# Sums of squares of eleven norms: two fp32r parts in place of one fp32 operand, in a two-block transformer kernel

## The reference

```python
def rms_norm(x, w):
    x32 = x.astype(f32)
    y = x32 * lax.rsqrt(jnp.mean(x32 * x32, axis=-1, keepdims=True) + EPS)
    return (y * w.astype(f32)).astype(x.dtype)
...
def head_rmsnorm(o, w):
    B, S, H, dv = o.shape
    of = o.astype(jnp.float32)
    y = of * lax.rsqrt(jnp.mean(of * of, axis=-1, keepdims=True) + NORM_EPS)
    return y.reshape(B, S, H * dv) * w.astype(jnp.float32)
```

## Time and profile before

| | us |
|---|---|
| median of three runs | 1858.04 |
| lowest and highest | 1856.46 and 1858.89 |
| the profiled execution | 1859.46 |
| its span | 1857.7 |
| PE busy in it | 1821.0 |

### The profile page before, as it was taken

One profiled execution on the slowest core, in us unless ns is written; L12 is line 12 of the kernel. 1 busy time (PEld: TensorE's weight loads), 2 busy tenths in 40 slices (PEclk: granted clock), 3 DMA queues, 4 the chain that ended last, 5 costly groups with the idle time before them and its releaser, 6 DMA issues.

```text
span 1857.7 us, 22226 instructions
## 1 busy us (share of the span) xinstructions
PE 1821.0 (98%) x8534; PEld 1434.4 (77%) x8534; DVE 826.2 (44%) x1381; ACT 521.2 (28%) x1038; POOL 947.5 (51%) x510
## 2 busy tenths in 40 slices
PE   7999989999999999999999999999999999999998
PEld 5885556888888887777887888677788878888886
DVE  6328754522023335435004473666645476305533
ACT  3125654221012112212104232555510132222222
POOL 5443132766666666455665555443466635444442
PEclk9999999999999999999999999999999999999999
DMA  5620101222222233121322222211122213222221
GB/s 183 212 70 26 48 23 46 102 99 94 102 91 102 91 102 113 67 81 69 110 96 75 76 73 80 68 60 69 58 102 91 102 63 107 91 102 92 101 94 65
DMA packets 46729, 162.55 MB, mean 88 GB/s; under 512 B 5392, under 2 KB 6736, under 8 KB 46241
## 3 DMA queue, kind: packets, MB, share of 16 engines
q1 hardware_dynamic: 43088, 154.52, 23.8%
q10 hardware_dynamic: 3537, 6.61, 1.2%
HBM read 158.13 MB, written 2.12 MB: 86 GB/s over the span
## 4 chain that ended last, share of the span: by engine, by line
PE 91%; DVE 4%; ACT 2%; issue 1%; DMA 0%; POOL 0%; SPq 0%; DVEq 0%; ACTq 0%; POOLq 0%
PE bank L728 90%; PE bank L1063 1%; DVE att_l_t L2048 0%; DVE att_l_t L2028 0%; DMA x_sb<-in_x 0%; DVE h_lo L1746 0%; ACT att_l_t L1561 0%; POOL w_lo_t L2295 0%; ACT sb_e L1600 0%; ACT sq L1283 0%; DVE att_l_t L2050 0%; DVE sq_sum L1692 0%; ACT sb_e L1599 0%; ACT h_hi L1392 0%; ACT att_pt L1573 0%
## 5 line engine op out<-in xcount | busy, mean ns | idle before, releaser
L2295 POOL TENSOR_TENSOR w_lo_t<-w_raw,w_hi_t 128x1024 fp32r<-128x1024 f32 x275 | 691.6, 2515 | 187.6 <-ACT w_hi_t L1359 169.7
L2293 POOL TENSOR_SCALAR w_hi_t<-w_raw 128x1024 fp32r<-128x1024 f32 x215 | 235.3, 1094 | 662.7 <-PE bank L728 633.7
L728 PE MATMUL bank<-h_hi,w_hi_t 128*128 128x512 f32 (+1 forms) x1060 | 433.4, 409 | 10.5 <-ACT h_hi L1392 9.1
L728 PE MATMUL bank<-h_hi,w_lo_t 128*128 128x512 f32 (+1 forms) x1060 | 415.2, 392 | 0.0
L728 PE MATMUL bank<-h_lo,w_hi_t 128*128 128x512 f32 (+1 forms) x1060 | 409.2, 391 | 0.4 <-DVE h_lo L1746 0.3
L728 PEld LDWEIGHTS bank<-h_hi,w_hi_t 128*128 128x128 f32 x1060 | 201.0, 190 | 70.4 <-issue 26.3
L728 PEld LDWEIGHTS bank<-h_lo,w_hi_t 128*128 128x128 f32 x1060 | 199.8, 189 | 46.2 <-issue 3.2
L728 PEld LDWEIGHTS bank<-h_hi,w_lo_t 128*128 128x128 f32 x1060 | 201.1, 190 | 40.7 <-issue 1.2
L728 PE MATMUL bank<-hid_hi,w_hi_t 128*128 128x512 f32 x432 | 168.0, 389 | 0.0
L728 PE MATMUL bank<-hid_lo,w_hi_t 128*128 128x512 f32 x432 | 168.0, 389 | 0.0
L728 PE MATMUL bank<-hid_hi,w_lo_t 128*128 128x512 f32 x432 | 168.0, 389 | 0.0
(11 more groups left out here) (308 smaller groups left out, 2676.9 us busy)
## 6 DMA issues: line engine op xcount, KB each, us to landing
w_raw<-in_w SPq DMA_DIRECT2D x276, 512.0 KB, 3.2
y<-in_w SPq DMA_DIRECT2D x6, 512.0 KB, 5.9
x_sb<-in_x SPq DMA_DIRECT2D x4, 512.0 KB, 7.7
x_sb<-in_x ACTq DMA_DIRECT2D x2, 1024.0 KB, 5.4
out_y<-x_sb SPq DMA_DIRECT2D x8, 256.0 KB, 2.1
u_raw<-in_w SPq DMA_DIRECT2D x2, 512.0 KB, 6.1
toep<-table ACTq DMA_DIRECT2D x4, 256.0 KB
decay<-in_decay SPq DMA_DIRECT2D x1, 1024.0 KB, 4.8
```

The lines of the kernel that those rows point to most:

```text
L728: return pe.matmul(out, lhs, rhs, start=start, stop=stop, **kw)
L2293: pool.tensor_scalar(hi, raw, 1.0, 0.0, ALU.mult, ALU.add).then_inc(*did("w_hi", i))
L2295: pool.tensor_tensor(lo, raw, hi.bitcast(F32), ALU.subtract).then_inc(*did("w_lo", i))
```

## The change

`IN_PARTS` names the eleven norms. For these

- DVE also adds the last square (it matters for n2 and fpre, which have eight), so that `sq_sum` is complete;
- at the step "norm" ACT copies `sq_sum` into an fp32r buffer (the high part; it uses one of the two places of `sq`), and DVE subtracts it from `sq_sum` in place (the low part);
- PE waits for the low part (`sq_lo`) and multiplies both parts by ones in fp32r into the same bank, two matmuls.

`sq_parts` is a view of the memory of `sq` and `sq_sum` with the type fp32r. ACT's next squares wait for the bank of sums where they would overwrite a high part.

```diff
--- before.py
+++ after.py
@@ -320,6 +320,7 @@
 HI_AT = {}
 for i in ACT_HI:
     HI_AT.setdefault(LAST_USE[BEHIND[i]], []).append(i)
+IN_PARTS = ("cq", "n2", "fpre") + tuple((name, h) for name in ("ret", "gla") for h in range(4))
 UNNORMED = ("n1", "n2", "pre_u", "fpre")
 FROM_U = (("rq", 0), ("rk", 0), ("rq", 1))
 FIRST_LOADS = 2
@@ -327,7 +328,7 @@
 
 SEMAPHORES = """x_in0 x_in1 x_in2 x_in3 x_back ones_set r_cols mask_in mixer_in kv_in ksw_in kr_in zeros table_out sq_pe const_in wqb_in misc_in late_in alibi_in alibi_s bias_in y_out
 w_hi wa_hi w_lo slot_used v_chain s_chain sq_s sq_v rstd rstd_used ms_lo
-h_t h_hi hy_hi u_hi h_ready x_pool p_chain bias_v bcast_v gate_v nsa_v cmpx cmp_s cmp_v att_l att_n att_exp att_p att_tr att_done
+h_t h_hi hy_hi u_hi h_ready x_pool p_chain bias_v bcast_v gate_v nsa_v sq_hi sq_lo cmpx cmp_s cmp_v att_l att_n att_exp att_p att_tr att_done
 lora mla_k mla_q mla_rot sb_sp sb_exp sb_a sb_pe conv_y y_ready p_conv hid_s hid x_ready ret_s ret_a ret_d ret_done sil
 o_ready o_hi m_ready gla_v gla_s gla_kd gla_st gla_a gla_done gla_t prod gate_s merged merged_hl q_s swa_s ft lo_t table last_t last_x""".split()
 
@@ -388,8 +389,11 @@
     par = sb("par", [P, -(-NPCOL // 32) * 32])
     small = sb("small", [P, 4, 8])
     r_col = small[:, :, 7]
-    ones = sb("ones", [P, P])
+    ones_r = sb("ones", [P, P], F32R)
+    ones = ones_r[:].bitcast(F32)
     ident = sb("ident", [P, P])
+    with nc.sbuf_tensor("sq_parts", [P, 3, T], F32R) as sq_r:
+        pass
     sq = sb("sq", [P, 2, T])
     sq_sum = sb("sq_sum", [P, T])
     rstd_t = sb("rstd_t", [P, 3, T])
@@ -620,6 +624,9 @@
         if step[0] == "sq":
             sq_use[step[1:]] = len(sq_use)
     sq_uses = list(sq_use)
+
+    def sum_high(key):
+        return sq_r[:, sq_use[(key, len(norms[key][0]) - 2)] % 2]
 
     def rstd(key):
         _, parts, cols, *_ = norms[key]
@@ -757,6 +764,11 @@
                                              False, True))
                 return
             out = take(("ms", key))
+            if key in IN_PARTS:
+                pe.wait_ge(*after("sq_lo", key))
+                mm(out[:], ones_r[:], sum_high(key), True, False)
+                fill(("ms", key), mm(out[:], ones_r[:], sq_r[:, 2], False, True))
+                return
             if n_src == 1:
                 pe.wait_ge(*after("sq_s", key, 0))
                 rhs = sq[0:parts, sq_use[(key, 0)] % 2, 0:cols]
@@ -1255,7 +1267,7 @@
             u = sq_use[(key, c)]
             if u >= 2:
                 k2, c2 = sq_uses[u - 2]
-                if len(norms[k2][0]) == 1 or c2 == KD - 1:
+                if len(norms[k2][0]) == 1 or c2 == KD - 1 or (k2 in IN_PARTS and k2 != key):
                     act.wait_ge(*ms_full(k2))
                 else:
                     act.wait_ge(*after("sq_v", k2, max(c2, 1)))
@@ -1323,6 +1335,9 @@
                     act.wait_ge(*evacuated(("ms", key, hf)))
                     act.activation(r_half, r_half, ACT.Exp, scale=-0.5).then_inc(*did("rstd", key, hf))
                 return
+            if key in IN_PARTS:
+                act.wait_ge(*after("sq_v", key, len(srcs) - 1))
+                act.activation(sum_high(key), sq_sum[:], ACT.Copy).then_inc(*did("sq_hi", key))
             act.wait_ge(*full(("ms", key)))
             r = ring_at.get(key, 0)
             if r >= 3:
@@ -1679,7 +1694,7 @@
         def squares(key, c):
 
             srcs, parts, cols, *_ = norms[key]
-            if 0 < c < KD - 1:
+            if 0 < c < KD - (key not in IN_PARTS):
                 own("sq_s", key, c)
                 b = [sq[0:parts, sq_use[(key, x)] % 2, 0:cols] for x in (c - 1, c)]
                 if c == 1:
@@ -1715,7 +1730,12 @@
         last_h = None
         for step in ORDER:
             stage = step[0]
-            if stage == "bias_tables":
+            if stage == "norm" and step[1] in IN_PARTS:
+                key = step[1]
+                own("sq_hi", key)
+                dve.tensor_tensor(sq_r[:, 2], sq_sum[:], sum_high(key).bitcast(F32), ALU.subtract)\
+                   .then_inc(*did("sq_lo", key))
+            elif stage == "bias_tables":
                 dve.memset(y[:, 5:8], 0.0).then_inc(*did("zeros"))
                 for n, (c0, w) in enumerate(TAB):
                     dve.wait_ge(*full(("tab", n)))
```

## The result

| | before | changed |
|---|---|---|
| median, us | 1857.25 | 1898.9 |
| lowest and highest | 1856.38 and 1858.89 | 1897.28 and 1901.24 |
| span of the profiled execution | 1857.7 | 1899.4 |

The changed kernel is slower by 2.25%: the ratio is 1.0225, with a 95% interval of 1.0212 to 1.0238, or 41.7 us between the medians. The forecast was 1904, in a range of 1886 to 1918.

What follows compares the result with a forecast made beforehand. PE, busy for 98% of the span, was taken as the bound. Waits of 37.1 us less 6.2 saved make 30.9, plus 15 for the clock is 45.9; on the median of 1858.04 that gave 1904, range 1886 to 1918.

Steps and rivals of the forecast that it cites:

- PE's saving: At the eleven norms' sums, fp32r matmuls replace fp32: 3.7 us in nine norms, 2.5 in n2 and fpre, 6.2 saved.
- The waits: At all eleven norms PE waits for ACT's high copy and DVE's subtraction: 37.1 us, or 30.9 less the saving.
- POOL's hold: In retention, gla 3 and fpre, POOL's w_lo starts first and holds DVE's subtraction until some 0.55 us behind its end.
- Rival 2: The subtraction isn't held by POOL: five waits 0.9 us shorter, fpre's 1.9; 1897.5 us, chance 0.08.
- The race in gla: In gla 0 to 2 DVE's subtraction starts 0.09 us ahead of POOL's w_lo; wait 2.21 each, 4.56 if POOL is first.
- Rival 1: The waits of gla 0 to 2 are lost to POOL: 2.35 us more each, clock falls fully; 1914, chance 0.15.
- n2: Wait at norm n2: 1.11 us if DVE precedes POOL's w_hi, 2.07 if not; the middle, 1.6, was taken.
- The clock: Half-clock stretches behind new waits: six long at 2.0 us, three of 2.2 us at 1.0; 15 us, bounds 5 and 27.
- The border that the forecast drew: PE gaps of 1.72 us and more were followed by half clock, one of 1.53 wasn't; the border lies between.
- Rival 3: The clock isn't lowered behind the new waits of PE: 1889 us, chance 0.08.
- Nothing taken back: Every wait falls where PE ran without a gap, so none of the 30.9 us later is recovered.
- Rival 5: Waits partly given back by a later gap that another engine causes: near no change 0.02, a part (about 1880) 0.04.

Runs made afterwards that it cites:

- doubled copy: The changed kernel with a second, superfluous high copy ahead of the real one in gla 0, 1 and 2; 1912.99 us against 1857.64 for the kernel before, ratio 1.0302.
- short waits alone: The kernel before with the change only in norms cq, n2 and gla 0, 1 and 2; 1865.84 us against 1857.64, ratio 1.0045.
- long waits alone: The kernel before with the change only in retention 0 to 3, gla 3 and fpre; 1895.33 us against 1857.64, ratio 1.0205.

## Why the prediction was right, point by point

- **PE's saving** of 6.2 us: measured alone 6.1, with an interval of 3.7 to 8.4, and 5.4 in the trace. It is right in the main. The forecast took 0.41 for every head, but behind ret 0 and ret 2 a shorter sum uncovers the copy of kf. In the changed kernel this doesn't show, since the waits cover that copy.
- **The waits**: 37.1 forecast, 36.1 measured, every long one within 0.1 us. The method was to take each link (copy, table load, copy, subtraction, hand-over to PE) from its row and to put them in sequence in the order of the queues.
- **POOL's hold**: 0.54 behind the end of w_lo in the earlier trace rows, 0.54 in the changed kernel. It made the wait of retention 4.49 instead of about 3.6. The run with the copy ahead of the table load and the one with the doubled copy show it in both directions. Rival 2 is out.
- **The race in gla**, forecast with a margin of 0.09 us for DVE: won by 0.11 in all three heads. Rival 1 is out; the doubled copy shows its price, 1913 against the 1914 forecast for it.
- **n2** was the only wait that was mis-sized: I took the middle between two orders, and DVE was first by 0.06 us (1.10, as the lower end said).
- **The clock**: 15 us forecast, 14.1 measured in the profile, but made up otherwise, so that the sum fits is luck. The long waits cost 2.35 each, not 2.0, since four of six were followed by 6.8 us and not by 3.4; the short ones cost nothing, not 1.0. The border that the forecast drew, between gaps of 1.53 and 1.72 us, didn't hold: in the changed kernel a gap of 1.71 and three of 2.02 were followed by full speed. Rival 3 is out, since the clock did fall behind all six long waits.
- **Nothing taken back**: this was wrong, by 2.1 us. Behind fpre 0.7 us were taken back, by the gap at 1528 that the prediction passed over, and cq's 1.4 vanished among half-clock stretches that fell otherwise. Rival 5 is true to this small part.

The forecast is 5 us too high. The waits make 1.0 of it, the clock 0.9, what was taken back 2.1, and 0.8 is the median of before, which was 1858.0 when the forecast was made and is 1857.25 with one more run.

## What to carry to other kernels

An operand that is made just in time at the old place of its use is not free, however cheap its instructions are: look in the queue of each engine that makes it for what stands ahead, above all the evacuation of the very matmuls that were meant to cover it. Moving the making ahead, or the use behind the next independent matmuls, takes the wait away, but then look at what the removed time had covered (here a copy of 0.6 us under a sum of 0.86).

A wait on an instruction that a second engine can hold up is a step: 0.66 us of delay cost 2.31. Where PE is the bound, price a gap with the clock that may fall behind it, and place instructions that lie within a tenth of a microsecond of a competitor as if they might lose.

## What was not expected of the hardware

How the granted clock follows the gaps of PE, counted over the eleven profiles of this case (the kernel before, the changed one, nine variants):

| gap of PE, us idle | where | followed by half clock |
|---|---|---|
| 1.53 to 1.54 | attention of the second block (to 1171 before) | 0 of 11 |
| 1.60 | cq, where it waits for parts | 0 of 4 |
| 1.71 to 1.72 | attention of the first block (to 167 before) | 2 of 11 |
| 1.89 to 1.95 | parts made early: ret 0, gla 2 (in two kernels), fpre | 1 of 4 |
| 2.02 to 2.08 | changed kernel 0 of 3, copy ahead of the table load 6 of 8, short waits alone 1 of 3 | 7 of 14 |
| 2.17 to 2.18 | norm y1 (to 264 before) | 10 of 10 |
| 2.43 | for DVE's h_lo (to 1481 before) | 11 of 11 |
| 4.33 to 4.36 | changed kernel 6, doubled copy 9, long waits alone 6, copy ahead of the table load 1 | 22 of 22 |

Longer gaps were followed by half clock more often, but equal gaps were not treated alike, so the length of the gap doesn't decide by itself. In seven of the profiles the clock even fell within 2 us behind a gap of 0.92 us (at 250), the last of four pauses of PE of 1.3, 1.3, 1.1 and 0.9 us since 215. What decides stays open. For a forecast, a gap of 2 us cost 0 or 1.7 us here, and one of 4.3 us between 1.7 and 2.9.
